# Both pairs of value products by Strassen's scheme, with GpSimd making the low half of T2

## The reference

```python
act = jax.nn.gelu(jnp.einsum('td,tkd->tk', xb, u[eb]))
return jnp.einsum('tk,tkd->td', gb * act, v[eb])
```

## Time and profile before

| | |
|---|---|
| median of 3 runs | 1782.0 us (1780.98 to 1785.47) |
| the profiled execution, its time | 1781.31 us |
| its span in the trace | 1779.5 us, so 1.8 us lie around it |
| PE busy | 1722.6 us, 97% of the span |
| DVE busy | 1460.9 us, 82% |
| ACT busy | 723.3 us, 41% |
| POOL busy | 381.7 us, 21% |
| granted TensorE clock, mean | 0.993 of full speed |

### The profile page before, as it was taken

How to read it: one execution, slowest core, us unless ns; L and a number is a source line. 1 busy time by engine, 2 the same in 40 slices (tenths; PEclk the granted TensorE clock), 3 DMA queues, 4 the chain that set the end, 5 groups by cost and what they waited for, 6 DMA issues and landing times.

```text
span 1779.5 us, 24820 instructions
## 1 busy us (share of the span) xinstructions
PE 1722.6 (97%) x8316; PEld 1397.7 (79%) x8316; DVE 1460.9 (82%) x2495; ACT 723.3 (41%) x903; POOL 381.7 (21%) x171
## 2 busy tenths in 40 slices
PE   5999999999999999999999999999999999999997
PEld 4774688888777788878888888888888888888885
DVE  7898779999699953388888788887878888787889
ACT  2451433332389962344343343433334343343430
POOL 1000264664300014431111111111111111111102
PEclk8999999999999999999999999999999999999999
DMA  9544210245369997654444444444444444444431
GB/s 382 220 161 165 115 43 1 101 142 191 123 192 284 283 287 257 233 195 149 148 144 148 165 147 159 145 141 150 149 169 147 149 146 147 154 147 166 150 122 70
DMA packets 137358, 293.07 MB, mean 165 GB/s; under 512 B 8256, under 2 KB 73920, under 8 KB 134624
## 3 DMA queue, kind: packets, MB, share of 16 engines
q1 hardware_dynamic: 135600, 287.34, 47.2%
q0 software_dynamic: 1424, 4.85, 0.8%
q10 hardware_dynamic: 288, 0.29, 0.1%
HBM read 237.93 MB, written 54.53 MB: 164 GB/s over the span
## 4 chain that ended last, share of the span: by engine, by line
PE 79%; DVE 13%; issue 3%; ACT 1%; DMA 1%; POOL 1%; DVEq 0%; SPq 0%; ACTq 0%; POOLq 0%
PE bank L1018 25%; PE bank L1020 25%; PE bank L1019 25%; DVE arena L1699 1%; DVE arena L1693 1%; DVE acc L1699 1%; DMA wbuf<-ada_w_dram 1%; DVE acc L1693 1%; PE bank L993 1%; PE bank L1097 1%; DVE arena L1361 1%; DVE u_lo L1686 1%; PE bank L1142 1%; PE bank L1146 1%; DVE u_lo L1908 1%
## 5 line engine op out<-in xcount | busy, mean ns | idle before, releaser
L1018 PE MATMUL bank<-h_hi,u_hi 128*128 128x512 f32 x1272 | 501.4, 394 | 5.7 <-ACT w_raw L872 2.5
L1020 PE MATMUL bank<-h_hi,u_lo 128*128 128x512 f32 x1272 | 495.6, 390 | 0.0
L1019 PE MATMUL bank<-h_lo,u_hi 128*128 128x512 f32 x1272 | 495.0, 389 | 0.0
L1018 PE MATMUL bank<-v_hi,w_hi 128*128 128x512 f32 x932 | 362.5, 389 | 0.0
L625 POOL TENSOR_TENSOR u_lo<-u_raw,u_hi 128x1024 fp32r<-128x1024 f32 x62 | 158.6, 2558 | 784.4 <-ACT u_hi L878 776.2
L1018 PEld LDWEIGHTS bank<-h_hi,u_hi 128*128 128x128 f32 x1272 | 238.8, 188 | 56.6 <-issue 6.8
L1020 PEld LDWEIGHTS bank<-h_hi,u_lo 128*128 128x128 f32 x1272 | 238.7, 188 | 50.8
L1019 PEld LDWEIGHTS bank<-h_lo,u_hi 128*128 128x128 f32 x1272 | 239.0, 188 | 49.0 <-issue 0.7
L1018 PEld LDWEIGHTS bank<-v_hi,w_hi 128*128 128x128 f32 x932 | 174.9, 188 | 36.4
L847 ACT ACTIVATE v_hi<-v_raw 128x1024 fp32r<-128x1024 f32 x124 | 128.2, 1057 | 185.2 <-PE bank L1020 140.0
L1019 PE MATMUL bank<-v_lo_y,w_hi 128*128 128x512 f32 x496 | 192.9, 389 | 0.0
(11 more groups left out here) (243 smaller groups left out, 2532.6 us busy)
## 6 DMA issues: line engine op xcount, KB each, us to landing
u_raw<-ut_dram SPq DMA_DIRECT2D x128, 512.0 KB, 4.0
v_raw<-v_dram SPq DMA_DIRECT2D x128, 512.0 KB, 3.3
gate_in<-gates_dram SPq DMA_DIRECT2D x64, 512.0 KB, 3.2
wbuf<-ada_w_dram SPq DMA_DIRECT2D x10, 2048.0 KB, 14.9
early_dram<-arena SPq DMA_DIRECT2D x64, 256.0 KB, 2.3
gates_dram<-wbuf SPq DMA_DIRECT2D x4, 4096.0 KB, 16.0
w_raw<-early_dram SPq DMA_DIRECT2D x64, 256.0 KB, 2.8
gates_dram<-arena SPq DMA_DIRECT2D x3, 4096.0 KB, 16.0
```

The costliest lines, as they stand in the source:

```text
L1018: pe.matmul(out, a_hi, b_hi, start=(k == 0), stop=False)
L1019: pe.matmul(out, a_hi, b_lo, start=False, stop=False)
L1020: return pe.matmul(out, a_lo, b_hi, start=False, stop=(k == n - 1))
```

## The change

Both pairs of a group now go by Strassen's scheme. A block product is a sum over both pairs (`for r in range(2)`), six matmuls for a token tile in one bank:

```diff
-            def product(b, t, k, n, w, v):
-                w_of, v_of = w_slots(w, w + 1), v_slots(v, v + 1)
-                t_of = slice(t * P, (t + 1) * P)
-                return thrice(bank[b][:, :], k, n, ((w_of[0][:, t_of], w_of[1][:, t_of]), v_of))
+            def product(b, t, w, v, opens=True, closes=True):
+                for r in range(2):
+                    w_of = tuple(of[:, r, w, t * P:(t + 1) * P] for of in (w_hi, w_lo))
+                    v_of = tuple(of[:, r, v, :] for of in (v_hi, v_lo))
+                    k = r + (0 if opens else 1)
+                    mm = thrice(bank[b][:, :], k, k + (1 if closes and r else 2), (w_of, v_of))
+                return mm
```

PE's order in a group becomes:

```diff
                 late_inputs(i, T_EARLY + 2, 2, BANK_U)
-                pe.wait_ge(s_wlo, i * 5 + 1)
-                pe.wait_ge(s_vlo, i * 5 + 1)
+                pe.wait_ge(s_wlo, i * 4 + 1)
+                pe.wait_ge(s_vlo, i * 4 + 2)
                 for t in range(2):
+                    product(BANK_P1 + t, t, A11, B11, opens, closes)
...
                 for t in range(2):
+                    product(4 + t, t, S3, T3).then_inc(s_vmm, 1)
+                late_inputs(i, T_EARLY + 3, 2, BANK_U)
+                pe.wait_ge(s_wlo, i * 4 + 3)
                 for t in range(2):
+                    product(6 + t, t, A12, B21).then_inc(s_vmm, 1)
                 for t in range(2):
                     pe.wait_ge(s_acc, i * SUMS + (1 + t))
+                    product(4 + t, t, S4, B22).then_inc(s_vmm, 1)
+                pe.wait_ge(s_wlo, i * 4 + 4)
+                pe.wait_ge(s_vlo, i * 4 + 4)
+                product(BANK_P6, 0, S2, T2, opens, closes)
+                pe.wait_ge(s_acc, i * SUMS + 3)
+                product(6, 1, S2, T2).then_inc(s_vmm, 1)
+                for t, b in enumerate((7, 4)):
+                    pe.wait_ge(s_acc, i * SUMS + (4 + t))
+                    product(b, t, S1, T1).then_inc(s_vmm, 1)
                 for t in range(2):
                     pe.wait_ge(s_acc, i * SUMS + (6 + t))
+                    product(5 + t, t, A22, T4).then_inc(s_vmm, 1)
```

DVE's order in a group becomes (`firsts` and `group`, all the `+` lines in order; `value_sums` and `weight_sums` keep their four steps each, on both pairs at once, so twice as wide):

```diff
+            def firsts(i):
...
+                add_up(i, 1, acc_p7[:, halves[0]], 4)
+                add_up(i, 2, acc_p7[:, halves[1]], 5)
+                lo_w(i, 4, S2, S2 + 1, w_sum2[:, :, :])
+                ve.wait_ge(s_vlo, i * 4 + 4)
+
+            def group(i):
+                weigh_early(i, 1)
+                weigh(i, 1, 1)
+                firsts(i)
+                value_sums(i, 1)
+                weigh(i, 1, 3)
+                add_up(i, 3, acc_p2[:, halves[0]], 6)
+                add_up(i, 4, acc_p2[:, halves[1]], 7)
+                ve.wait_ge(s_wlo, i * 4 + 4)
+                weight_sums(i, 1)
+                add_up(i, 5, acc_p3[:, halves[0]], 4)
+                add_up(i, 6, acc_p3[:, halves[1]], 5)
+                lo_v(i, 5, B21, B22 + 1, v_b)
+                add_up(i, 7, acc_p6[:, :], 6)
+                lo_w(i, 5, A11, S3 + 1, w_a)
+                add_up(i, 8, acc_p5[:, halves[0]], 7)
+                add_up(i, 9, acc_p5[:, halves[1]], 4)
+                lo_v(i, 6, B11, T3 + 1, v_a)
+                lo_w(i, 6, S1, S4 + 1, w_14)
+                add_up(i, 10, acc_p4[:, halves[0]], 5)
+                add_up(i, 11, acc_p4[:, halves[1]], 6)
+                lo_w(i, 7, A12, A22 + 1, w_b)
+                lo_v(i, 7, T1, T4 + 1, v_14)
```

ACT makes S2 and T2 apart, into the slots that S3 and T3 leave, and POOL makes T2's low half between its two splits of u:

```diff
+            def seconds(i):
+                act.wait_ge(s_wlo, i * 4 + 3)
                 late_gelu(i, T_EARLY + 2, 2, BANK_U, 1)
                 late_hi_u(i, 0)
                 act.wait_ge(s_vmm, i * SUMS + 2)
+                act.wait_ge(s_ws, i * 4 + 3)
+                hi_w(S2, S2 + 1, w_sum2[:, :, :])
+                act.wait_ge(s_vs, i * 4 + 3)
+                hi_v(T2, T2 + 1, v_sum2[:, :, :])
                 late_gelu(i, T_EARLY + 3, 2, BANK_U, 3)
                 late_hi_u(i, 1)
...
+            def second_value_sum(i):
+                pool.wait_ge(s_vlo, i * 4 + 3)
+                pool.wait_ge(s_vhi, i * 4 + 4)
+                pool.tensor_tensor(slots(v_lo, T2, T2 + 1), v_sum2[:, :, :], slots(v_hi, T2, T2 + 1).bitcast(F32),
+                                   ALU.subtract).then_inc(s_vlo, 1)
...
             with pool.Fori(1, NQ) as i:
                 late_split_u(i, 0)
+                second_value_sum(i)
                 late_split_u(i, 1)
```

More of the change, by code:

```diff
@@ L59 @@
 NQ = (NGROUP - TAIL) // 2
-SUMS = 13
+SUMS = 11
 HALF = S // 2
 DH = D // 2
-A11, S3, A12, A22, S1, S2, S4, YA11, YA21, YA12, YA22 = range(11)
-B11, T3, B21, B22, T1, T2, T4, YB11, YB12, YB21, YB22 = range(11)
-XOPS, YOPS = 7, 4
+A11, S3, A12, A22, S1, S4 = range(6)
+B11, T3, B21, B22, T1, T4 = range(6)
+S2, T2 = S3, T3
+OPS = 6
 BANK_U, BANK_P1, BANK_P6 = 0, 1, 3
@@ L287, in last_w @@
             if m < TAIL:
-                return w_slots(*((A11, S3 + 1), (A12, A22 + 1), (YA11, YA21 + 1), (YA12, YA22 + 1))[m])
+                r, a = m // 2, m % 2 * 2
+                return tuple(t[:, r, a:a + 2, :].rearrange("p s n -> p (s n)") for t in (w_hi, w_lo))
             j = m - TAIL
@@ L523, in _ @@
             load_group(NQ - 1, ())
+            sp.wait_ge(s_vlo, 4 * NQ)
             sp.wait_ge(s_ulo, NT)
@@ L882, in _ @@
             hi_u(0, T_EARLY + 2)
[L883 to L889, removed]
+            act.wait_ge(s_vs, 2)
+            hi_v(B11, T3 + 1, v_a)
             late_gelu(0, T_EARLY + 1, 0, BANK_P6, 3)
             hi_u(0, T_EARLY + 3)
-            act.wait_ge(s_w, 3)
@@ L893, in _ @@
[L893 to L899 removed]
+            act.wait_ge(s_ws, 2)
+            hi_w(A11, S3 + 1, w_a)
+            act.wait_ge(s_vs, 4)
+            hi_v(T1, T4 + 1, v_14)
+            act.wait_ge(s_ws, 4)
+            hi_w(S1, S4 + 1, w_14)
+            hi_w(A12, A22 + 1, w_b)
+            def seconds(i):
+                act.wait_ge(s_wlo, i * 4 + 3)
@@ L1786, in _ @@
             ve.wait_ge(s_xs, 16)
+            ve.memset(acc_p6[:, :], 0.0).then_inc(s_zacc, 1)
+            ve.wait_ge(s_ulo, T_EARLY + GT)
             value_sums(0, 0)
-            lo_v(0, 1, (B11, T3 + 1), v_raw[:, 0, :])
-            lo_v(0, 2, (B21, B22 + 1), v_raw[:, 1, :])
-            for j in range(2):
-                lo_v(0, 3 + j, (YB11 + 2 * j, YB12 + 2 * j + 1), v_raw[:, 2 + j, :])
-            weigh(0, 0, 0)
-            weigh(0, 0, 1)
-            weight_sums(0, 0)
             for n in range(GT):
                 ve.wait_ge(s_spill[n], 16 * T_EARLY // GT)
-            lo_v(0, 5, (T1, T4 + 1), v_sums)
-            lo_w(0, 1, (A11, S3 + 1), w_raw[:, 0, :])
-            lo_w(0, 2, (S1, S4 + 1), w_sums)
-            lo_w(0, 3, (A12, A22 + 1), w_raw[:, 1, :])
-            weigh(0, 0, 2)
-            weigh(0, 0, 3)
-            lo_w(0, 4, (YA11, YA21 + 1), w_raw[:, 2, :])
-            lo_w(0, 5, (YA12, YA22 + 1), w_raw[:, 3, :])
-            ve.wait_ge(s_zacc, 4)
-            def group(i):
-                weigh(i, 1, 0)
-                weigh(i, 1, 1)
+            lo_v(0, 1, B21, B22 + 1, v_b)
+            lo_v(0, 2, B11, T3 + 1, v_a)
+            weigh_early(0, 0)
+            weigh(0, 0, 1)
+            weigh(0, 0, 3)
+            weight_sums(0, 0)
+            lo_w(0, 1, A11, S3 + 1, w_a)
+            lo_v(0, 3, T1, T4 + 1, v_14)
+            lo_w(0, 2, S1, S4 + 1, w_14)
+            lo_w(0, 3, A12, A22 + 1, w_b)
+            ve.wait_ge(s_zacc, 3)
+            def firsts(i):
                 if not isinstance(i, int) or i > 0:
```

348 lines of the change are left out of this document (134 added, 214 removed).

## The result

The changed kernel takes 1827.0 us in the median of four runs (1824.6 to 1828.7), beside 1783.4 for the kernel before on the same chip: ratio 1.0244, 95% interval 1.0223 to 1.0265. The forecast was 1824, range 1798 to 1845. The profiled span is 1823.6 us against 1779.5, so 44.1 us have to be found.

A forecast was written before the change was run, and what follows sets the result against it. PE was taken to bound the kernel before, DVE the changed loop. Start 7.9 + 28 periods x 1.34 - 3.5 at the end = 41.9 us more, span 1821.4; predicted median 1824 us, range 1798 to 1845.

The forecast's parts named there:

- What set the loop: Late loop: DVE without slack replaces PE as the bound, period 32.62 us instead of 31.28.
- DVE's 26.99 us: Late loop: DVE's work in a group after the change, summed start to start without losses, against 29.92 of PE.
- The three losses: Late loop: DVE stands still under POOL's three operations a group, 1.28 + 2.12 + 2.23 us.
- S2's low half with T2: Late loop: DVE's `lo_w` of S2 stands still while POOL makes T2's low half, loss 1.28 us.
- step four: Late loop: the last step of `value_sums` on DVE stands still under POOL's second split of u, loss 2.12 us.
- `weigh_early`: Late loop: this DVE operation stands still under POOL's first split of u, ending at 11.95 instead of 9.72, loss 2.23 us.
- the walk: Late loop: one group timed operation by operation from PE's first u matmul, closing at a period of 32.62 us.
- PE's three waits: Late loop: PE waits for DVE's adds 3, 5 and 7 in each group, 0.91 + 1.10 + 0.69 = 2.70 us.
- The start: Before the late loop's group 1: more DVE work and POOL operations make it begin 7.9 us later, between 4 and 12 possible.
- the loads hide: Late loop: rows are freed some 5 us at the least before use, for transfers of 3 to 4 us.
- The end: Group 29 and tail: 1.36 us shorter group, first read 1.0 less, one addition 1.14 less, together -3.5 us.
- the old tail: After the loop: the 10.93 us piece behind POOL's last four subtractions stays as in the kernel before.

The follow-up runs named there:

- all three POOL operations narrow: Changed kernel with T2's low half and both late-loop splits of u on POOL cut to 16 elements a partition instead of 1024: 1745.7 us.
- the first split narrow: Changed kernel with POOL's first split of u in each late-loop group cut to 2 of 128 columns: 1811.8 us, period 32.14.
- Narrow T2: Changed kernel with POOL's T2 low half cut to 16 elements instead of 1024, its wait and place kept: 1759.4 us, period 29.92.
- the narrow second split: Changed kernel with POOL's second split of u in each late-loop group cut to 2 of 128 columns: 1762.3 us, period 30.38.
- the trains: Kernel without the computation: nine trains of DVE operations, POOL asking once in each (twice in the ninth); each train of eight two-SBUF-input operations took 11.31 us.
- S: In the kernel of DVE trains alone, a DVE operation with two SBUF inputs of 1024 elements; three undisturbed take 3.48 us.

## Why the prediction was right, and where a step failed

**What set the loop: right.** PE gives the pace up, DVE takes it, and each group is longer by DVE's standing still under POOL. With all three POOL operations narrow the loop runs at 29.92 us, 132 matmuls at 0.2267 as counted. DVE's 26.99 us, as counted, fit under these 29.92 with 2.93 to spare, and everything beyond these 2.93 is lost time.

**The three losses: the sum right, one term in the wrong place.** Forecast: S2's low half with T2 1.28, step four 2.12, `weigh_early` 2.23, together 5.63. Measured: S2's low half 0.77 (1.45 - 0.68) and the wait for T2 2.28, together 3.05; step four 2.07; `weigh_early` nothing; adds 1 and 2 0.2, where the second waits for its bank, since DVE comes to it sooner than in the walk. Together 5.3, and 26.99 + 5.3 = 32.3 for a measured 32.45. The step that failed is "POOL's first split asks at 8.09, works 8.54 to 10.95, and `weigh_early` frees DVE at 11.95 instead of 9.72: loss 2.23". POOL asked at 8.2 but worked from 10.3 to 12.7, two DVE operations later. Then two things followed that the walk didn't have: the first split's work lay mostly under adds 1 and 2, free, and its end pushed T2's low half back. T2 was asked for at 12.8 as forecast, but POOL got to it later, DVE's S2 came in between, and DVE then waited for the whole 2.4 us of T2 with nothing to do. So `value_sums` started at 15.5, where 15.63 was forecast: two errors that cancelled, and that the period came out so near was luck in this part. The test is the first split narrow: by my term it had to give 1765, it gave 1811.8.

**Not additive.** Narrow T2 gives back 68 us, the narrow second split 65, both splits and T2 81. One reason is that the losses hang together: without T2's operation the second split no longer meets step four and costs only the 0.76 us of L1737, so that DVE's sum is 26.99 + 0.76 = 27.8. The other is the floor: that sum lies below the 29.92 of PE, and what is below is PE's. Without the second split it is 26.99 + 3.05 + 0.2 = 30.2 (measured 30.38), which leaves little more to gain. In the kernel before, DVE stood still as well, and it cost nothing.

**PE's three waits: right in place, near in size.** For adds 3, 5, 7: 0.91, 1.10, 0.69 forecast. Three rows of PE in order of time, of one group:

```profile
1227.73 0.50 PE L1002 MATMUL bank<-v_hi,w_hi 128*128 128x512 f32 x1 [0.40 <-DVE acc L1725]
...
1231.59 0.50 PE L1002 MATMUL bank<-v_hi,w_hi 128*128 128x512 f32 x1 [0.82 <-DVE acc L1725]
...
1234.98 0.50 PE L1002 MATMUL bank<-v_hi,w_hi 128*128 128x512 f32 x1 [0.38 <-DVE acc_p L1725]
```

The idle before is counted from the end of the matmul before, which overlaps; start to start the waits are about 0.7, 1.1 and 0.65.

**The start: 10.1 instead of 7.9.** The walk's step for it was `value_sums` of group 0 at 795.5, and from there 17.0 us to group 1. `value_sums` began at 797.63, and 17.1 us later, at 814.7, group 1. DVE had made A12's low half by 789.15 (788.5 forecast) and then stood idle, waiting for the rows of early results that SP loads:

```profile
791.33 2.95 DVE L1710 TENSOR_TENSOR w_raw<-w_raw,gate_in 128x1024 f32<-128x1024 f32 x1 [2.18 <-DMA w_raw<-early_dram]
```

From 791.33 to `value_sums` it had no gap. The prediction had put the loads at nothing ("ACT (14 us a group) and the loads hide"); here 2.18 us of them did not.

Something else in this stretch was not in the sum. Block product P1 of group 0 waits until 784.18 (783.5 forecast). PE in order of time, then the busy time by engine after that wait and after the like one in the tail:

```profile
784.18 0.79 PE L1002 MATMUL bank<-v_hi,w_hi 128*128 128x512 f32 x1 [4.55 <-DVE w_lo L1720]
784.77 0.63 PE L1003 MATMUL bank<-v_lo,w_hi 128*128 128x512 f32 x1
785.20 0.63 PE L1004 MATMUL bank<-v_hi,w_lo 128*128 128x512 f32 x1
```
```profile
784.50:787.30 2.80, 2.80 (x7) 2.15 (x7) 2.72 (x2) 1.95 (x3) 0.00 (x0) 0.50 0.94 363
...
1791.60:1795.00 3.40, 3.40 (x8) 2.72 (x9) 0.91 (x1) 0.00 (x0) 0.00 (x0) 0.50 0.00 0
```

The granted clock is 0.50, the lower of the two levels (1.2 GHz), and matmuls start 0.43 us apart instead of 0.227, thirteen of them before the clock is back: 2.6 us. P7 ended later by this, ACT made the high halves of S2 and T2 only behind it, and S2's low half then met POOL's work on T2 (1.70 us instead of 0.68). How much of the 2.2 us this makes, beside the wait for the loads, no run shows. The gaps of 1.1 us and less in the loop left the clock at 1.00, as forecast.

**The end: +1.3 instead of -3.5.** Group 29 is as forecast. The tail is not. POOL and then DVE in order of time; POOL's four subtractions, and the first of them alone:

```profile
1773.74 17.70 POOL L640 TENSOR_TENSOR h_lo<-v_raw,h_hi 128x1024 fp32r<-128x1024 f32 x4
1773.74 7.77 POOL L640 TENSOR_TENSOR h_lo<-v_raw,h_hi 128x1024 fp32r<-128x1024 f32 x1
```
```profile
1774.63 2.35 DVE L1885 TENSOR_TENSOR acc<-acc,row_gate 128x1024 f32<-128x1024 f32 x2
1776.90 1.22 DVE L1885 TENSOR_TENSOR row_g<-row_g,row_gate 128x1024 f32<-128x1024 f32 x1
1778.04 1.22 DVE L1885 TENSOR_TENSOR acc<-acc,row_gate 128x1024 f32<-128x1024 f32 x1
1779.29 6.64 DVE L1891 SCALAR_TENSOR_TENSOR u_raw<-u_raw,acc 128x1024 f32<-128x1024 f32 x2
```

POOL's last four subtractions, 4 x 2.4 us of work, take 17.70. The first alone waits 5.4 us, while DVE runs the last of four L1882 and four L1885 through undisturbed (until 1779.25); then they alternate with L1891, both at 3.3 to 3.4. PE waits for all four until 1791.58, 4.6 us, and starts again at the lower clock.

The prediction carried the old tail over: "the long piece of 10.93 us behind POOL's last four subtractions stays". It did not. In the kernel before, POOL had asked 0.31 us into DVE's third subtraction of the same kind (L1908, now L1882), just as here. DVE in order of time, in the kernel before:

```profile
1734.24 10.33 DVE L1908 TENSOR_TENSOR u_lo<-w_raw,u_hi 128x512 fp32r<-128x512 f32 x1
```

There POOL worked at once and did all four in 9.46 us, and this subtraction stood still meanwhile; here DVE went first. Why the same meeting went the other way isn't shown.

**The sum.** The total is so near, 44.1 us for a forecast of 41.9, because misses cancel, and this is luck too: the start is 2.2 us longer than forecast, the 28 periods together 4.8 shorter (32.7 instead of 37.5), the end 4.8 longer.

## What to carry to other kernels

When an operation is moved to an engine that excludes the bottleneck's feeder while it works, as POOL does with DVE's operations on two SBUF inputs, price it as time taken from both, and set the sum against the slack, which is pace less work: the two splits of u cost nothing where DVE was idle for 5.5 us of a group, and the second of them 65 us, beside T2's operation, where DVE's work left 2.9. Such losses are cured by order, not by waits: put operations that read PSUM where POOL works, and give the engine that already waits the operation itself (this gave 1768, below both kernels, where moving the semaphore wait gave 7 us). And a walk that gives the right period can have a wrong term in it; the run that removes that one term tells.

## What the runs showed of the hardware

**Who goes first at a boundary is not one rule here.** In the trains and in the earlier trace rows POOL goes in at the next boundary even if DVE's next operation is queued. (It does so before L1753 too, but there DVE waits for its own last result.) In every group of the loop it is passed over twice, by `weigh_early` and L1702, and waits 2.08 us; in the tail it is passed over by five operations and waits 5.4. In the tail of the kernel before it was DVE that was passed over, by four operations of POOL (L1908 above). It is not the time of the request alone: in the kernel with all three operations narrow, POOL asked 0.26 us into L1711 (`weigh_early` there), as early in the operation as in the trains (0.23), and still came in only after the next one. DVE, then POOL, in order of time:

```profile
1201.26 1.22 DVE L1711 TENSOR_TENSOR w_raw<-w_raw,gate_in 128x1024 f32<-128x1024 f32 x1
1202.39 0.69 DVE L1703 TENSOR_TENSOR w_raw<-w_raw,gate_in 128x512 f32<-128x512 f32 x1
...
1201.52 1.64 POOL L618 TENSOR_TENSOR u_lo<-u_raw,u_hi 128x16 fp32r<-128x16 f32 x1 [18.63 <-ACT u_hi L877]
```

An operation of 0.22 us of work lasted 1.64. Nor is it a full DVE queue, by the trains. Nor is it the kind of the passing operations: `weigh_early` and L1702 multiply in place, with a gate that is read strided, but L1700, which does so too, stood still under POOL when it followed step four; the first to pass in the tail, L1882, subtracts into another tile, as S does; and `weigh_early` itself stood still in the loop's first group, where POOL had asked at 774.79:

```profile
775.60 3.41 DVE L1710 TENSOR_TENSOR w_raw<-w_raw,gate_in 128x1024 f32<-128x1024 f32 x1
```

What decides stays open. The Trainium skill (SBUF — State Buffer, "Who interferes with whom") says that the pair is kept for an instruction. The trains agree (one stretch of 2.1 us each); the rows of the loop and of the two tails show that one engine can also go first several times in a row while the other waits.

**A wait of 4.6 us before a matmul costs more than itself.** Both times, at the start of the loop and in the tail, it was followed by a granted clock of 0.50, and at the start PE needed 2.6 us more for the next thirteen matmuls.
